# Expert weight slots of four row blocks by 1024 columns in place of eight row blocks by 512

## The reference, cut to what matters

```python
gt = jnp.minimum(xb @ w_gate[e] + b_gate[e], 7.0)
up = jnp.clip(xb @ w_up[e] + b_up[e], -7.0, 7.0)
y  = (gt * sigmoid(1.702 * gt) * (up + 1.0)) @ w_down[e] + b_down[e]
# y is weighted by the token's softmax weight and summed over its 4 experts
```

## Time and profile before

| | us |
|---|---|
| time, median of 3 runs | 2595.86 (2594.13 to 2597.4) |
| span of the profiled execution | 2593.4 |
| the median minus that span | 2.5 |
| TensorE busy | 2266.3 (87%) |
| expert products L820, busy | 1471.6 |
| expert products L820, idle before them | 189.6 |
| weight loads, each 2048 KB, to landing | 7.7 |

### The profile page before, as it was taken

One profiled execution on the slowest core, in us unless ns is written; L12 is line 12 of the kernel. 1 busy time (PEld: TensorE's weight loads), 2 busy tenths in 40 slices (PEclk: granted clock), 3 DMA queues, 4 the chain that ended last, 5 costly groups with the idle time before them and its releaser, 6 DMA issues.

```text
span 2593.4 us, 40962 instructions
## 1 busy us (share of the span) xinstructions
PE 2266.3 (87%) x15570; PEld 1967.9 (76%) x15571; DVE 827.6 (32%) x2385; ACT 543.5 (21%) x1148; POOL 166.1 (6%) x121
## 2 busy tenths in 40 slices
PE   7999988999958779799979788799999788999992
PEld 2446666665438779799979788799999778999992
DVE  0103567422352222233322222233233222333334
ACT  1003222222011211122221121122222112222211
POOL 0000000000320000000000000000000000000002
PEclk8998555558968889899999899899999889999996
DMA  9202300017344664677774575577777566787741
GB/s 292 65 0 80 144 15 15 13 53 272 109 145 176 218 229 166 202 260 280 265 246 163 177 268 206 204 266 274 265 261 272 189 222 231 265 287 271 262 170 66
DMA packets 263232, 490.51 MB, mean 189 GB/s; under 512 B 32955, under 2 KB 42683, under 8 KB 263116
## 3 DMA queue, kind: packets, MB, share of 16 engines
q1 hardware_dynamic: 251164, 467.74, 51.1%
q0 software_dynamic: 11952, 21.01, 3.1%
HBM read 484.43 MB, written 25.76 MB: 197 GB/s over the span
## 4 chain that ended last, share of the span: by engine, by line
PE 86%; issue 8%; DVE 3%; DMA 2%; ACT 1%; SPq 0%; POOLq 0%; DVEq 0%; POOL 0%; ACTq 0%
PE bank L820 57%; PE bank L680 5%; PE bank L597 4%; PE bank L713 4%; PE bank L699 2%; PE bank L812 2%; PE bank L766 2%; PE bank L724 2%; PE bank L872 1%; DMA att<-in_w_ada 1%; PE bank L573 1%; PE bank L594 1%; ACT att L1028 1%; PE bank L661 1%; PE bank L689 1%
## 5 line engine op out<-in xcount | busy, mean ns | idle before, releaser
L820 PE MATMUL bank<-att,ring 128*128 128x128 f32 (+4 forms) x12288 | 1471.6, 283 | 189.6 <-issue 189.6
L820 PEld LDWEIGHTS bank<-att,ring 128*128 128x128 f32 x12288 | 1462.0, 195 | 197.2 <-issue 197.1
L1379 DVE TENSOR_SCALAR att<-bank,pa 128x256 f32<-128x256 f32 x256 | 123.9, 484 | 567.7 <-PE bank L820 567.7
L1018 ACT ACTIVATE att<-att 128x256 f32<-128x256 f32 x256 | 106.7, 417 | 548.6 <-DVE att L1379 548.6
L1401 DVE TENSOR_SCALAR pa<-bank,pa 128x256 f32<-128x256 f32 x256 | 123.8, 484 | 241.7 <-PE bank L820 241.7
L1022 ACT ACTIVATE att<-bank,pa 128x256 f32<-128x256 f32 x256 | 121.4, 474 | 350.9 <-PE bank L820 350.9
L1005 ACT ACTIVATE att<-bank 128x512 f32<-128x512 f32 x66 | 39.5, 598 | 505.0 <-PE bank L812 505.0
L1368 DVE COPY pa<-att 128x24 f32 x32 | 5.8, 181 | 430.6 <-ACT att L1022 429.8
L680 PE MATMUL bank<-att 64*128 64x128 f32 (+1 forms) x192 | 136.6, 816 | 0.0
L499 POOL DMA_INDIRECT moe_output<-att,master x37 | 58.7, 1585 | 1038.8 <-ACT att L1028 1001.2
L713 PEld LDWEIGHTS bank<-att,pa 128*128 128x128 f32 x480 | 115.0, 336 | 1.6 <-ACT pa L967 0.8
(11 more groups left out here) (241 smaller groups left out, 1368.7 us busy)
## 6 DMA issues: line engine op xcount, KB each, us to landing
ring<-in_w_gate SPq DMA_DIRECT2D x64, 2048.0 KB, 7.7
ring<-in_w_up SPq DMA_DIRECT2D x64, 2048.0 KB, 7.7
ring<-in_w_down SPq DMA_DIRECT2D x64, 2048.0 KB, 7.7
att<-in_w_ada SPq DMA_DIRECT2D x2, 4096.0 KB, 22.7
ring<-in_w_ada SPq DMA_DIRECT2D x4, 2048.0 KB, 12.7
att<-in_w_ada SPq DMA_DIRECT2D x4, 2048.0 KB, 13.3
ring<-in_w_in SPq DMA_DIRECT2D x2, 2048.0 KB, 10.2
ring<-in_w_out SPq DMA_DIRECT2D x1, 4096.0 KB, 25.1
```

Of the source, the lines that this page charges most:

```text
L820: last = nc.tensor.matmul(bank[f % 4][:, 0:n], w[:, k, c:c + P], src[:, k, 0:n], start=(k == 0), stop=(k == KC - 1))
L1018: nc.scalar.activation(sgm[:, f % 2, :], gcl[:, f % 2, :], ACT.Sigmoid, scale=1.702).then_inc(s_sig, 1)
L1379: nc.vector.tensor_scalar(gcl[:, f % 2, :], bank[f % 4][:, 0:SL], bcur[:, 0, f:f + 1], 7.0, ALU.add, ALU.min).then_inc(s_gdr, 1)
```

## The change

A slot now holds 4 row blocks of all 8 column blocks. The two slots of a matrix both wait for the eighth product of that matrix (before: for the fourth and for the eighth), and product f=0 waits for the first slot at k=0 and for the second at k=4 (before: f=0 and f=4 waited). The source of a load is 512 rows of 4 KB in place of 1024 pieces of 2 KB.

```diff
 def expert_load(j, i, e):
-    m, c0 = j * SC // KC, j * SC % KC * P
-    sp.wait_ge(s_mm, i * 24 + SC * (j + 1))
-    sp.dma_start(ringf[:, j * SC * D:(j + 1) * SC * D].rearrange("p (k n) -> p k n", k=KC),
-                 a[names[m]][0, e, :, c0:c0 + SC * P].rearrange("a (k p) n -> p (a k) n", p=P)).then_inc(s_w[j], 16)
+    m, k0 = j // 2, j % 2 * SC * P
+    sp.wait_ge(s_mm, i * 24 + KC * (m + 1))
+    sp.dma_start(ring[:, j * SC:(j + 1) * SC, :],
+                 a[names[m]][0, e, k0:k0 + SC * P, :].rearrange("a (k p) n -> p (a k) n", p=P)).then_inc(s_w[j], 16)
...
-def products(m, f, src, n):
-    slot, c = (m * KC + f) // SC, (m * KC + f) % SC * P
-    w = ringf[:, slot * SC * D:(slot + 1) * SC * D].rearrange("p (k n) -> p k n", k=KC)
+def products(before, m, f, src, n):
     for k in range(KC):
-        last = nc.tensor.matmul(bank[f % 4][:, 0:n], w[:, k, c:c + P], src[:, k, 0:n],
+        if f == 0 and k % SC == 0:
+            pe.wait_ge(s_w[2 * m + k // SC], before * 16 + 16)
+        last = nc.tensor.matmul(bank[f % 4][:, 0:n], ring[:, m * KC + k, f * P:(f + 1) * P], src[:, k, 0:n],
                                 start=(k == 0), stop=(k == KC - 1))
     last.then_inc(s_mm, 1)
...
-    def weights(m, f):
-        if f % SC == 0:
-            pe.wait_ge(s_w[(m * KC + f) // SC], i * 16 + 16)
```

More of the change, by code:

```diff
@@ L830, in expert @@
                 for f in range(KC):
-                    weights(0, f)
                     if f < 4:
@@ L835, in expert @@
                         pe.wait_ge(s_gdr, i * 8 + f - 3)
-                    products(0, f, hTe, n)
+                    products(i, 0, f, hTe, n)
                 for f in range(KC):
-                    weights(1, f)
                     if f < 4:
@@ L842, in expert @@
                         pe.wait_ge(s_udr, i * 8 + f - 3)
-                    products(1, f, hTe, n)
+                    products(i, 1, f, hTe, n)
                 pe.wait_ge(s_gd, i + 2)
@@ L849, in expert @@
                 for f in range(KC):
-                    weights(2, f)
                     if f < 4:
@@ L856, in expert @@
                         pe.wait_ge(s_pr, i * 8 + 8)
-                    products(2, f, prod, n)
+                    products(i, 2, f, prod, n)
                 for g in range(4):
```

## The result

The kernel with the new slots takes 2610.72 us (median of 4 runs, 2610.07 to 2614.69), against 2596.63 us for the kernel before beside it: ratio 1.0051, 95% interval 1.0037 to 1.0066. It is 14 us slower; 11 were forecast. The span went from 2593.4 to 2608.3 us. The size fits. The place doesn't: the page of the kernel after, read beside the earlier trace rows, shows where the time went.

A forecast was written before the change was run, and what follows sets the result against it. TensorE's expert products bound the kernel, waiting only for branches and code fetches, never DMA. Single gathers 4.4 plus double gathers 6.8 made 11 us on 2595.86, so 2607 us; 8-in-10 range 2589 to 2624.

The forecast's parts named there:

- signs of being wrong: Gather landing stays near 6 us; a product waits for a slot; idle before the eleven experts changes over 1 us.
- Parts 1 to 3: Weight loads: later slot release, earlier need of the second half (19 us of cover), 4 KB pieces; each costs 0.
- Part 4, the gathers at 11 us: Next expert's row gathers wait for both gate loads, delaying L812: 4.4 us for single gathers plus 6.8 for double.
- a software transfer stands behind what the hardware queue already holds on each engine: On the DMA engines, the gather waits for both gate loads to drain, 5.1 us more.
- The landing of 2.2 us: Kernel's last gather, no load in flight, landed 2.2 us after issue; the median was 5.9.
- round robin: Rival: gathers share the DMA engines from issue or some 2 us later, all hidden; 2596 to 2599 us, chance 0.31.
- 1.7 us for a double gather: Before each of four wide experts, the second gather makes L812 late by 1.7 us, bounds 0 and 3.2.
- The scatter: Beside the down pair, lands at 1119.1 to 1120.4, before VectorE needs it at 1123.23: cost 0.
- Part 5, the code stalls, costed at 0 with an upper bound of 8 us: TensorE's eleven code-fetch stalls now run beside a pair of loads: 0 to 0.74 us each, taken as 0.
- The code pages: Rival: shifted code addresses remove two short TensorE stalls, gaining 15 us; 2580 to 2590 us, chance 0.12.

The follow-up runs named there:

- Experiments 7 and 8: One copy of the expert's code, for 128 columns, in the kernel before and in the kernel after: 2353.14 and 2354.82 us.
- experiments 2 and 3: Kernel after with only the down matrix as before: 2598.67 us; kernel before with only the down matrix changed: 2615.87 us.
- the fifth kernel: Kernel before with its second down load of the next expert held until that expert's first gate product: 2566.15 us, ratio 0.9877.

## Why the prediction was right, and for which wrong reason

The time lay where it was forecast, 2611 against 2607, and slower was the likeliest sign. The sum behind it was wrong: 11 us for the gathers measured 0, 0 for the code stalls measured 17, and the errors nearly cancelled. That the number came out was luck, and two of the prediction's own signs of being wrong showed it: the gathers landed after 7.6 us and not 11, and nine of the eleven stalls moved by more than 1 us.

- **Parts 1 to 3** (release, need, transfers at nothing) held. Narrow experts keep 48.07 us, no product waits for a slot, SP's pairs stand as drawn up. Experiments 7 and 8 show that these parts cost nothing.
- **Part 4, the gathers at 11 us**, was wrong: it measured 0. The step that failed is "a software transfer stands behind what the hardware queue already holds on each engine". It rested on gather and scatter beginning as the load drained, at two distances. The rule does not hold at either. After the change the gather begins 4.2 to 4.4 us after its issue (3.7 to 4.1 before) with over 5 us of load still to come, and from then on shares, as the earlier trace rows had shown for the stores. The landing of 2.2 us, from which I took what a load costs, was that of a gather that moved no rows: 144 packets, 0.00 MB. Of the rivals, round robin described it best, in its form with a fixed delay: some 2 us later when a load is in full flow, then its share. For the scatter the delay is not fixed. Its first packet came 2.6 to 2.9 us after its issue under the load before and 4.7 to 5.6 under the pair, still in the middle of the load; why was not tried. The arithmetic on top (1.7 us for a double gather) had no cause left. The longest gather took 9.0 us, so the cover of the doubles was thin, but it held.
- **The scatter** was rightly costed at 0. Forecast were 11 us and more to its landing; this one took 10.0 and landed at 1124.5, and the copy that waits for it came at 1129.56 (L1381 there).
- **Part 5, the code stalls, costed at 0 with an upper bound of 8 us**, measured 17 us: +1.6 us on average over the eleven, +2.0 over the nine at a change of width. The bound came from comparing the loop's entry, beside a pair of loads, with a later stall beside one: 18.36 and 17.62 us. That pair had been issued 4.6 us before TensorE stopped, and had all but drained (11 packets from 780 to 780.6) when the entry's second fetch came, 8.8 us after the stop. In the loop the pair is issued about 2 us before the stop, so its second half lies right over the second fetch. The same number of loads in flight was not the same position in the chain of fetches.
- **The code pages** as a rival for a gain had no part: experiments 2 and 3 each change TensorE's code again, and their stalls follow the down loads; the two short stalls stayed in every kernel that has a load beside them.

I missed a third thing, the largest: the single load of the kernel before was already in the way of the first fetch. In the kernel before every stall had a load beside it, so no row showed what a stall is without one. That was worth 29 us.

## What to carry to other kernels

A stall for code is a chain of dependent small DMAs, and they suffer from bulk loads that nobody waits for: before moving a load, look at what else asks the DMA engines for something short at that moment, instruction fetches included, and move bulk loads with slack to where the engines that branch are running in code they hold. When a bound is taken from a comparison of two stalls, line up when the load was issued and drained against each link of the chain, and not only whether a load was there. And if a delay begins when a load drains, look for a case where the two differ before calling it a queue.

## What the runs showed of the hardware that was not expected

- A code fetch (one 16 KB packet) came later under a weight load. The first fetch of the stall ahead of the 176-column expert began 4.4 us after the stop with one load and 1.7 us without; over the eleven stalls of the loop it was 2.1 to 3.3 us later in the kernel before than in the fifth. The second fetch there began 5.6 us after the first under the pair, 3.2 to 3.4 us without a load over it; over the nine at a change of width it was 5.1 to 6.8 us under the pair and 3.1 to 4.0 in the fifth kernel. The packet itself, once it began, took about as long with a load as without: 1.0 to 1.3 us for the first, up to 2.3 for the later of two that overlap. So the time is lost before the fetch begins; where is not shown.
- A gather was delayed by about the same: from issue to first packet 1.6 us without a load, 3.7 to 4.1 us with a load that flowed for some 4 us more (before), and 4.2 to 4.4 us with a pair that flowed for some 9 us more (after). A scatter's first packet came after 2.1 us without a load, 2.6 to 2.9 with the one load before and 4.7 to 5.6 with the pair.
- With two loads in flight at a stall, 2 KB pieces cost more than 4 KB pieces (212.1 against 206.2 us of idle time, 2619 against 2611 us); with one load in flight they cost the same (189.6 and 189.3 us). Why was not tried.
- TensorE ran through narrow experts of one width, turn after turn of the loop, without a packet of q8: none from 1073 to 1350 us in the kernel before, and with a single copy of the expert's code none from 812 us to the end.
